# Decayed-product recurrence beside projection units: scans, the order of a half unit, and which groups of PSUM the products use

## The reference

```python
lff = log(max(lb + (1 - lb) * sigmoid(f_fwd), F_MIN))        # likewise lfb
b = cumsum(l, axis=time)                                     # within a chunk
o_inter = (q * exp(b)) @ state
attn[t, s] = sum_k q[t, k] * k[s, k] * exp(b[t, k] - b[s, k])   # s <= t
o = o_inter + attn @ v
new_state = exp(b_last) * state + (k * exp(b_last - b)).T @ v
```

## Time and profile before

| | us |
|---|---|
| median of 3 runs | 3149.23 (3148.26 to 3149.43) |
| profiled execution | 3152.26 |
| its span, first to last instruction | 3150.5 |
| mean granted TensorE clock | 0.989 of full |

### The profile page before, as it was taken

How to read it: one execution, slowest core, us unless ns; L and a number is a source line. 1 busy time by engine, 2 the same in 40 slices (tenths; PEclk the granted TensorE clock), 3 DMA queues, 4 the chain that set the end, 5 groups by cost and what they waited for, 6 DMA issues and landing times.

```text
span 3150.5 us, 45245 instructions
## 1 busy us (share of the span) xinstructions
PE 3037.7 (96%) x18354; PEld 2466.8 (78%) x18354; DVE 1544.4 (49%) x1947; ACT 1186.1 (38%) x1937; POOL 1065.5 (34%) x509
## 2 busy tenths in 40 slices
PE   8999999999999999999999899999999999999999
PEld 6867688888888776788887677788888777788887
DVE  4364446462233586623312765467753765454420
ACT  3255421212123445423233434543332434544431
POOL 1302032323344212045453221245545221145553
PEclk9999999999999999999999999999999999999999
DMA  7201024342222233344332212046665212033332
GB/s 217 44 6 41 1 73 130 86 141 60 68 61 66 44 108 87 88 118 110 101 97 83 63 48 69 20 122 187 188 192 156 68 48 70 18 91 100 94 100 88
DMA packets 442379, 279.77 MB, mean 89 GB/s; under 512 B 113610, under 2 KB 419516, under 8 KB 441788
## 3 DMA queue, kind: packets, MB, share of 16 engines
q1 hardware_dynamic: 442172, 276.87, 31.5%
HBM read 274.73 MB, written 2.10 MB: 88 GB/s over the span
## 4 chain that ended last, share of the span: by engine, by line
PE 68%; DVE 3%; POOL 3%; ACT 3%; issue 2%; DMA 1%; SPq 0%; DVEq 0%; ACTq 0%; POOLq 0%
PE ps L693 46%; PE ps L1420 4%; POOL WL L2448 2%; PE ps L946 2%; PE ps L1496 2%; PE ps L1518 2%; PE ps L1489 1%; PE ps L1235 1%; PE ps L885 1%; PE ps L1561 1%; ACT WH L1816 1%; PE ps L1245 1%; PE ps L1262 1%; PE ps L1303 1%; PE ps L1592 1%
## 5 line engine op out<-in xcount | busy, mean ns | idle before, releaser
L2448 POOL TENSOR_TENSOR WL<-RAW,WH 128x1024 fp32r<-128x1024 f32 (+2 forms) x344 | 828.2, 2408 | 1691.7 <-ACT WH L1816 1682.5
L693 PE MATMUL ps<-HH,WH 128*128 128x512 f32 x2136 | 710.8, 370 | 13.8 <-POOL WL L2448 12.0
L693 PE MATMUL ps<-HH,WL 128*128 128x512 f32 x2136 | 704.5, 367 | 0.0
L693 PE MATMUL ps<-HL,WH 128*128 128x512 f32 x2136 | 701.8, 366 | 0.0
L1816 ACT ACTIVATE WH<-RAW 128x1024 fp32r<-128x1024 f32 (+2 forms) x344 | 356.0, 1035 | 411.3 <-PE ps L693 257.6
L693 PEld LDWEIGHTS ps<-HH,WH 128*128 128x128 f32 x2136 | 368.9, 189 | 96.8 <-POOL WL L2448 20.8
L693 PEld LDWEIGHTS ps<-HH,WL 128*128 128x128 f32 x2136 | 367.6, 189 | 67.3
L693 PEld LDWEIGHTS ps<-HL,WH 128*128 128x128 f32 x2136 | 367.0, 188 | 66.2
L2745 DVE SCALAR_TENSOR_TENSOR XT<-RAW,CS,XT 128x1024 f32<-128x1024 f32 x77 | 140.7, 1827 | 31.2 <-DMA RAW<-in_w_ada 30.2
L693 PE MATMUL ps<-FH,WH 128*128 128x512 f32 x308 | 120.5, 391 | 0.9 <-POOL WL L2448 0.8
L693 PE MATMUL ps<-FH,WL 128*128 128x512 f32 x308 | 120.0, 390 | 0.0
(11 more groups left out here) (493 smaller groups left out, 5529.2 us busy)
## 6 DMA issues: line engine op xcount, KB each, us to landing
RAW<-in_w_in SPq DMA_DIRECT2D x122, 512.0 KB, 3.9
RAW<-in_w_ada SPq DMA_DIRECT2D x96, 512.0 KB, 3.9
RAW<-in_w_up SPq DMA_DIRECT2D x88, 512.0 KB, 4.2
RAW<-in_w_in SPq DMA_DIRECT2D x72, 256.0 KB, 3.7
RAW<-in_w_mod SPq DMA_DIRECT2D x32, 512.0 KB, 3.7
RAW<-in_w_down SPq DMA_DIRECT2D x32, 512.0 KB, 4.1
WMOD<-in_w_mod SPq DMA_DIRECT2D x8, 1024.0 KB, 14.0
RAW<-in_w_branch SPq DMA_DIRECT2D x16, 512.0 KB, 3.4
```

Source lines behind the costliest of these rows:

```text
L693: ins = nc.tensor.matmul(ps[0:width, t0:t0 + tn], a, b[:, k0 + k, tokens0 + t0:tokens0 + t0 + tn], start=first and k == 0 and i == 0, stop ...
L2448: nc.gpsimd.tensor_tensor(wl[:, 0:used], RAW[n % NRAW][:, 0:used], wh[:, 0:used].bitcast(F32), ALU.subtract).then_inc(*up(w_low))
```

## The change

- **Scans.** One scan of 512 per tile. Its factor `RUN` is 1, and 0 at the first token of each block of 128, where the sum starts anew.
- **Half unit.** TensorE issues the first half of the first beside unit (bi0ch) before item 0; every later half moves up by one item, and one half instead of two is left behind the spreads. ScalarE handles beside units at even items, and splits the next unit's weights (`ahead`) ahead of the turned product.
- **Exponentials.** Those of items 0 and 1 move in `first_units` between the SiLU of bg 1 and the copy of bq 0. `decayed` makes KP before QP, and only QP waits for bq's copy.
- **Groups.** `open_beside`: transposes, rotated products, and the head sums of mixer_c are written to columns 512 to 1023 of the group of the unit that is under way. All other groups of this stretch, the head sums of mixer_a among them, are taken from a table, `LEVEL_BANKS`, in order of opening, relative to the first.
- **Total.** The sum of pair 0 moves from item 12, ahead of `turn2`, to item 13.

```diff
@@ -343,7 +343,7 @@
         HMASK = place("HMASK", [P, 10 * P], R0 + 32, I32)
-        ONE_ROW = place("ONE_ROW", [P, P], R0 + 37)
+        RUN = place("RUN", [P, SEQ], R0 + 62)
         QPX = place("QPX", [P, 2, SEQ], R0 + 38)
@@ -566,6 +566,7 @@
         SPAN = len(LEVELS) + 1
+        LEVEL_BANKS = "0123012301230123012302302010231302120312301230123"
         FIRST_UNITS = [("bff", 0), ("bfb", 0), ("bff", 1), ("bfb", 1), ("bg", 0), ("bg", 1), ("bq", 0)]
@@ -1379,41 +1380,50 @@
+            def open_beside(key, unit):
+                g = led.slot(unit)
+                uses[g] += 1
+                led.events["slot", key] = g
+                led.events["use", key] = led.events["use", unit] = uses[g]
+                return psum[g][:, SEQ:2 * SEQ]
             def gemm2(l, name, j, new=None, place=None):
-            def turned(l, name, j):
+            def turned(l, name, j, unit, turn):
...
                     got(("2", l, name, 0))
-                    ps = open_group(("2", l, name[:-2]))
+                    ps = open_beside(("2", l, name[:-2]), unit)
                     for tb in range(NXB):
...
                 elif name in ("aq", "cq"):
-                    head_sums(l, a, j)
+                    key = ("2", l, a, j, "sum")
+                    head_sums(l, a, j, open_group(key, turn()) if a == "a" else open_beside(key, unit))
                     if a == "a":
...
                         pe.wait_ge(const2_in, 16)
-                        ps = open_group(("2", l, a, j, "rot"))
+                        ps = open_beside(("2", l, a, j, "rot"), unit)
                         nc.tensor.matmul(ps[:, 0:SEQ], rot_32, QN2[a][:, j, :], start=True, stop=True).then_inc(
-            def beside(l):
+            def beside(l, turn):
...
                 for name, j in BESIDE:
+                    unit = ("2", l, name, j)
                     wh, wl = w_in2(l, name, j)
-                    ps = open_group(("2", l, name, j))
-                    held[0] = led.slot(("2", l, name, j))
+                    ps = open_group(unit, turn())
                     for half in range(2):
                         if half and before:
-                            turned(l, *before)
+                            turned(l, *before, unit, turn)
                         for k in range(KD // 2 * half, KD // 2 * (half + 1)):
@@ -1422,7 +1432,6 @@
                             given_back(("2", l, name, j))
-                            held[0] = None
                         yield
@@ -1548,13 +1557,19 @@
                         gemm2(l, name, j, place=None if n else led.slot((("2", l, "n", 0), "rows")))
-                other = beside(l)
+                order, first_bank = iter(LEVEL_BANKS), group[0]
+                def turn():
+                    return (first_bank + int(next(order))) % 4
+                other = beside(l, turn)
+                next(other)
                 for s, (t, d, i) in enumerate(ITEMS):
...
                         qp, kp = QP[n % 2], KP[n % 2]
-                        ps = open_group(("2", l, "lev", s))
+                        ps = open_group(("2", l, "lev", s), turn())
                         for c in range(NXB):
@@ -1565,7 +1580,7 @@
                     pe.wait_ge(to_pe, at(to_pe, ("2", l, "cross", s)))
-                    halves = [open_group(("2", l, "cross", s, h)) for h in range(2)]
+                    halves = [open_group(("2", l, "cross", s, h), turn()) for h in range(2)]
                     for n, (q, k, _, _) in enumerate(cross_blocks(d)):
@@ -1580,7 +1595,7 @@
                     td = s // SPAN
-                    ps = open_group(("2", l, "pv", td))
+                    ps = open_group(("2", l, "pv", td), turn())
                     for tb in range(NXB):
@@ -1594,11 +1609,13 @@
                     ins.then_inc(*up(product_ready, ("2", l, "pv", td)))
+                held[0] = led.slot(("2", l) + BESIDE[-1])
                 for j in range(4):
...
                     pass
+                held[0] = None
@@ -2278,6 +2295,9 @@
                         A(SZ2[j][:, :], ps[:, 0:SEQ], ACT.Silu).then_inc(*freed(key))
+                        if j:
+                            exponentials(l, 0)
+                            exponentials(l, 1)
                     else:
@@ -2309,16 +2329,18 @@
                         t = int(name[2])
-                        A(VH[:, :, t * P:(t + 1) * P], ps[:, 0:SEQ].rearrange("p (b v) -> p b v", v=P),
+                        A(VH[:, :, t * P:(t + 1) * P], ps[:, SEQ:2 * SEQ].rearrange("p (b v) -> p b v", v=P),
                           ACT.Copy).then_inc(*freed(key))
...
                             act.wait_ge(to_pe, at(to_pe, ("2", l, "rope", 3)))
-                        A(VN2[a][:, :, :].rearrange("p b v -> p (b v)"), ps[:, 0:SEQ], ACT.Copy).then_inc(*freed(key))
+                        A(VN2[a][:, :, :].rearrange("p b v -> p (b v)"), ps[:, SEQ:2 * SEQ], ACT.Copy).then_inc(
+                            *freed(key))
                 elif name in ("aq", "cq"):
...
                     ps = ready(key)
-                    A(HSUM[:, head_columns(a, j)], ps[:, 0:8], ACT.Copy).then_inc(*freed(key))
+                    c0 = SEQ if a == "c" else 0
+                    A(HSUM[:, head_columns(a, j)], ps[:, c0:c0 + 8], ACT.Copy).then_inc(*freed(key))
@@ -2348,8 +2370,6 @@
                 first_units(l)
-                exponentials(l, 0)
-                exponentials(l, 1)
                 for s, (t, d, i) in enumerate(ITEMS):
@@ -2363,10 +2383,12 @@
                         A(OSUM[t], ps[:, 0:SEQ], ACT.Copy).then_inc(*freed(key))
-                    if s % 2:
-                        if s > 1:
+                    if s % 2 == 0:
+                        name, j = BESIDE[s // 2]
+                        ahead(("2", l, name, j))
+                        if s:
                             turned(l, *BESIDE[s // 2 - 1])
-                        beside_kept(l, *BESIDE[s // 2])
+                        beside_kept(l, name, j)
                     if s == len(ITEMS) - 3:
@@ -3133,7 +3155,7 @@
                 step(V.tensor_tensor(x, x, ROPE[:, 0:SEQ], ALU.mult))
-                V.tensor_tensor(TB2[:, :], ps[:, 0:SEQ], ROPE[:, SEQ:2 * SEQ], ALU.mult).then_inc(*freed(key))
+                V.tensor_tensor(TB2[:, :], ps[:, SEQ:2 * SEQ], ROPE[:, SEQ:2 * SEQ], ALU.mult).then_inc(*freed(key))
                 own(key)
@@ -3219,13 +3241,13 @@
                 n, lv = 2 * d + t, level_number(s)
-                own(("2", l, "bq", t))
                 dve.wait_ge(act_out, at(act_out, ("2", l, "ee", s)))
...
                 tiles = [EE[e] for e in e_tiles(s)]
-                V.tensor_tensor(QP[lv % 2][:, :], QH[:, t, :], tiles[0][:, :], ALU.mult).then_inc(*up(to_pe))
-                V.tensor_tensor(KP[lv % 2][:, :], KK[:, n, :], tiles[-1][:, :], ALU.mult).then_inc(
+                V.tensor_tensor(KP[lv % 2][:, :], KK[:, n, :], tiles[-1][:, :], ALU.mult).then_inc(*up(to_pe))
+                own(("2", l, "bq", t))
+                V.tensor_tensor(QP[lv % 2][:, :], QH[:, t, :], tiles[0][:, :], ALU.mult).then_inc(
                     *up(to_pe, ("2", l, "kp", s)))
@@ -3274,7 +3296,8 @@
                     dve.wait_ge(product_ready, at(product_ready, ("2", l) + FIRST_UNITS[2]))
-                step(V.memset(ONE_ROW[:, :], 1.0))
+                step(V.memset(RUN[:, :], 1.0))
+                step(V.memset(RUN[:, 0:SEQ:P], 0.0))
                 lbv = LB[:, 24 + 4 * l:28 + 4 * l]
@@ -3287,9 +3310,7 @@
                     dve.wait_ge(act_out, at(act_out, ("2", l, "lf", n)))
-                    for c in range(NXB):
-                        cs = slice(c * P, (c + 1) * P)
-                        step(V.tensor_tensor_scan(FS[:, n, cs], ONE_ROW[:, :], LF[e][:, cs], 0.0, ALU.mult, ALU.add))
+                    step(V.tensor_tensor_scan(FS[:, n, :], RUN[:, :], LF[e][:, :], 0.0, ALU.mult, ALU.add))
                     ends = FS[:, n, :].rearrange("p (c t) -> p c t", t=P)[:, :, P - 1:P]
@@ -3309,10 +3330,10 @@
                         keep_level(l, s - 2)
-                    if s == 2 * SPAN:
-                        total(l, 0)
                     if s in (2 * SPAN, 2 * SPAN + 2, 2 * SPAN + 4, 2 * SPAN + 6):
                         turn2(l, (s - 2 * SPAN) // 2)
+                    if s == 2 * SPAN + 1:
+                        total(l, 0)
                 dve.wait_ge(act_out, at(act_out, ("2", l, "root", "a")))
```

## The result

The changed kernel takes 3127.76 us, median of 5 runs (3125.25 to 3130.98), against 3149.43 (3148.26 to 3150.49, 5 runs): a ratio of 0.9927, with a 95% interval of 0.9916 to 0.9939. The forecast was 3127.0. The profiled execution took 3128.52 us, 23.7 less than the one before (3152.26). The total agrees to a microsecond and a half; the terms do not, and the larger part of this text is about them.

The account below looks back on a forecast made before the run. TensorE, busy 3037.7 of 3150.5 us, was the bound, so only its ended waits count. Per layer 2.6 + 1.6 + 4.4 + 3.4 - 0.9 = 11.1 us, twice 22.2: profiled 3130.1, median 3127.0 us, range 3118 to 3139.

Parts of the forecast that it names:

- Step 1: Front, scans: 1.25 us per scan of 512, distances 4 us earlier, POOL held so bg1's low weights come 0.3 us later.
- Step 2: Front, moved exponentials: bi0ch's split and POOL's low half come later, a new TensorE wait of 1.65 us before the half unit.
- Step 3: Front, half unit before level 0: level 0 only 0.35 us later with 2.95 us of work behind it; gain 2.6 us.
- rival B: Front: the clock stays at 2.4 GHz over the new wait, 3.0 us better over both layers, 3124.0 us; chance 0.20.
- Step 4: Behind the front: splits ahead of turned products on ScalarE end four weight waits of up to 0.55 us, 1.6 us per layer.
- Step 5: Behind the front, PSUM groups: shared groups and the table remove 4.4 us per layer of waits for QNA and QNC.
- step 6: Around item 13: total after turn2 removes waits of 0.3 us and 1.6 us (DIAG) and a 1.5 us clock fall, 3.4 us.
- The 0.9 us put back for VectorE: Stretch with the rotations: VectorE becomes late next, costing 0.9 us per layer (0 to 2.8, and 1.5 of clock).
- rivals A: Items 12 to 18: VectorE is the bound, DIAG, clock and QNA waits stay, 5.8 us per layer; 3136.8 us, chance 0.17.
- C: Rival, stretch behind the front: the table only moves the waits, only the front acts; 3144.0 us, chance 0.09.
- D: Rival, items 13, 14, 16 and 17's values: groups wait for VectorE's rotation, 19.6 us per layer; slower, 3164.4 us, chance 0.04.
- The tail keeps its instructions: End of the stretch: instructions unchanged, one half unit fewer between the spreads and the scores; no time given for it.

Follow-up runs that it names:

- A: The kernel before with only the scans changed, four of 512 in place of sixteen of 128 per layer: 3152.3 us, ratio 1.000.
- C: The changed kernel with the exponentials of items 0 and 1 back behind the copy of bq0: 3129.73 us, ratio 0.9936.
- F: The changed kernel with ScalarE's split of bi0ch's weights ahead of the exponentials of items 0 and 1: 3119.93 us, ratio 0.9903.
- B: The changed kernel with PSUM groups in rotation again and each turned product in a group of its own: 3137.84 us, ratio 0.9969.
- D: The changed kernel with the total of the first pair back at item 12, ahead of `turn2`: 3130.07 us, ratio 0.9935.
- E: The changed kernel with each split of the next unit's weights back behind the turned product on ScalarE: 3133.06 us, ratio 0.9943.
- G: The changed kernel with the attention bias loaded behind the second unit of w_out, not the first: 3124.64 us, ratio 0.9912.
- H: The changed kernel with both the earlier bi0ch split and the later bias load: 3120.39 us, ratio 0.9899; measured again 3114.95 us, ratio 0.989.
- I: The changed kernel with the earlier bi0ch split, the later bias load and every table entry one group further: 3120.85 us, ratio 0.991.

## Why the prediction was right, and where its terms were off

The profiled executions differ by 23.7 us, and the landmarks on TensorE divide it: 0.4 up to bq0's end in the first layer, 12.8 from there to the first values' product of attention (1940.84 - 1781.05 against 1927.57 - 1780.61), 0.5 to bq0's end in the second, 13.5 in its stretch, and 3.5 lost behind it. The forecast had 11.4 per stretch from bq0's end (11.1 and the 0.3 by which bq0 was to be late), and nothing behind it.

Step 1. The scans take 1.22 to 1.23 us where I took 1.25. POOL was not held in the changed kernel: bg1 waits 2.13 us before and after, so the 0.3 us are 0. VectorE was the one to wait: its copy of four elements took 2.14 us, and a scan 3.28, under POOL's subtractions. The Trainium skill (SBUF — State Buffer, Who interferes with whom) has the first to issue block the other; by the trace POOL did block the copy, but the scan did not hold POOL, whose subtraction has its usual 2.34 from 1765.45, 0.2 us before the scan's end. In A, with 0.42 us of the scan left, it took 2.57.

Step 2 holds: forecast 1.65 us, measured 1.71. C shows what the step is worth: 1.1 us per layer over leaving the exponentials behind bq0, and F that a split put first would have saved 2.0 more.

Step 3. Half unit and level 0 came as forecast (4.65 us after bq0's end, forecast 4.60). The choice on the clock was wrong: what rival B assumed is what happened, and that alone is 1.5 us per layer that the sum left out. In ten stretches after a 1.71 us wait (both layers of the changed kernel and of B, D, E and G) the clock did not fall once, nor in C after 1.76. The rule of the Trainium skill (TensorE: Matmul & The Clock Gate) that I had set aside was the better guide: a short wait between full-rate units kept 2.4 GHz. The price of a fall was right (1.55 to 1.6 us). What was undersized is the wait: it costs 0.1 to 0.3 us beyond its idle time, 0.8 per layer. The edit "half unit" was not run without the rest; its part is read from the traces: up to level 2 the front gained 1.4 us (13.12 us from bq0's last matmul against 14.56) with one half unit (2.95) more in it, 4.4 us in all, as forecast (2.6, the 0.3 of bq0) with the clock's 1.5 on top.

Step 4 holds: 1.6 us of waits, 2.0 per layer at the first scores of E, and 2.6 by E's median, which holds scatter.

Steps 5 and 6. The waits for groups inside the stretch went, all of them, and with them more than the 4.4 us I gave them. The wait on DIAG, its clock and the 0.3 us on KP, 3.4 us in step 6, are not the order's alone: D, with the old order of `total` and the new groups, doesn't bring them back, and there the order is worth 0.4 us. B, with the new order and the old rotation, hasn't the wait on DIAG either, and has waits on QNA, QNC and XT in other places. So either edit is enough to end it, and which of them would have been enough in the kernel before is not shown. I took the instruction that stood in front of the late one for its only cause. Step 5 had checked the table's own entries and not two things outside it: the first scores behind it (1.36 us in the first layer), and the position of the round robin behind it (3.5 us in the last layer).

The 0.9 us put back for VectorE was 0: between level 0 and the last half unit TensorE waits nowhere, and the last steps of the rotations take 0.69 us each, not 1.37. So rivals A, C and D fall.

"The tail keeps its instructions" was true and priced wrongly. Its instructions were covered by 145 us of other work; with 13 us fewer in front, the transfer behind the bias shows, though A's waits of 2.4 and 1.4 us say that it does not need the shorter stretch. Of the gain at the first scores (13.3 and 14.8) the first values' product keeps 12.8 and 13.5.

So the mechanisms of the front, the weights and the groups were right, and the size came out to a microsecond by luck, by errors that cancel: too little for the clock, for the waits' own cost and for VectorE, too much for POOL's delay, nothing for the tail and the group at the end.

## What to carry to other kernels

When a change takes buffers out of a rotation, list what buffer each later user gets, far behind the change and in every layer: this one lost 3.5 us some 100 us downstream. A wait with no named releaser is worth holding against the ends of all reads on the other engines before thinking of anything rarer. And after shortening a stretch, ask which transfers in its shade were only just on time, and what large load lies ahead of them in the same queue.

## What the runs showed of the hardware that I had not expected

A wait of TensorE of 1.71 us left its clock up every time it was seen, while 1.59 us in front of the rotation made it fall; what ran on either side differed, so the length alone doesn't say. Not even the same place says: behind the wait of 2.13 us (once 2.35) in front of bg1 the clock fell in 25 of the 28 layers profiled, and stayed up in the second layers of G and H and the first of I, with the same instructions around it. In H (first profile; columns as in the earlier trace rows):

```profile
2463.70:2467.10 3.40, 3.40 (x17) 2.78 (x16) 3.37 (x2) 0.00 (x0) 2.13 (x1) 1.00 0.57 162
```

From bg1's start to bq0's last matmul that made 10.80 us instead of 12.38. So one fall costs 1.6 us, and a forecast can only give it a chance.

A copy of four elements on VectorE took 2.14 us instead of 0.17 while POOL subtracted, but POOL's memset of 1.85 us at 1782.21 let VectorE's differences and products run at their usual 0.68. Waits that are met already cost TensorE about 52 ns each: 96 more of them moved its first work by 5.0 us (6.62 to 11.62); the first 64 moved it by only 1.5 (from 5.07), where it would have waited for its input anyway.

The fastest of the kernels tried is H, 3120.39 and 3114.95 us in its two measurements, 1.0 and 1.1% under the kernel before; F alone, one line, is as fast within what can be told.
